# The in-place product of scattered expert weights and activations: order of the walk inside one instruction

## The reference, cut to what matters

```
s = einsum('thpc,hpnc->thpn', q, keys)           # 8 heads, 2 x 128 sub-keys
sv, si = top_k(s, 16);  cv, ci = top_k(all 16 x 16 sums, 16)
eid = e1 * 128 + e2;    g = softmax(cv)          # 16384 experts
a = einsum('td,thkd->thk', xb, u_tab[eid])
coef = g * gelu(a)
y = einsum('thk,thkd->td', coef, v_tab[eid])
```

## Time and profile before

| | us |
|---|---|
| median of the runs | 4343.08 |
| span of the profiled execution | 4344.9 |
| TensorE busy | 4117.4 (95%) |
| VectorE busy | 2832.0 (65%) |
| ScalarE busy | 1848.2 (43%) |
| GpSimd busy | 701.0 (16%) |
| L1320, 128 spreads | 167.3 |
| L474, 256 operations | 557.0 |

### The profile page before, as it was taken

The page is one execution under the profiler, slowest core; times in us unless marked ns, Lnnn a source line. Parts: engine busy times, 40 slices in busy tenths (PEclk is TensorE's granted clock), DMA queues, the critical chain, the costliest instruction groups (busy, mean ns, idle before and its releaser), DMA issues.

```text
span 4344.9 us, 90772 instructions
## 1 busy us (share of the span) xinstructions
PE 4117.4 (95%) x34860; PEld 4038.3 (93%) x34860; DVE 2832.0 (65%) x3745; ACT 1848.2 (43%) x2326; POOL 701.0 (16%) x397
## 2 busy tenths in 40 slices
PE   8999999989998899999999999999989988899998
PEld 7999999988998899999898899999989988899998
DVE  4554778789559965444545555878897489755444
ACT  4444444433443344444444444444434533344443
POOL 1211000054114510000002010000353045300000
PEclk9999999999999999999999999999999999999999
DMA  5455566644553356555554456666544533465554
GB/s 177 144 162 173 174 183 181 180 131 134 171 160 121 125 172 194 181 182 183 160 150 129 145 167 181 182 181 183 150 131 145 182 127 121 135 201 183 183 182 152
DMA packets 193647, 705.65 MB, mean 162 GB/s; under 512 B 21808, under 2 KB 22000, under 8 KB 193184
## 3 DMA queue, kind: packets, MB, share of 16 engines
q1 hardware_dynamic: 190224, 692.21, 51.8%
q0 software_dynamic: 3344, 12.32, 0.7%
HBM read 698.16 MB, written 6.29 MB: 162 GB/s over the span
## 4 chain that ended last, share of the span: by engine, by line
PE 78%; DVE 9%; POOL 5%; issue 4%; DMA 3%; ACT 1%; DVEq 0%; SPq 0%; POOLq 0%; ACTq 0%
PE ps L1424 24%; PE ps L1425 24%; PE ps L1426 24%; POOL hot L474 4%; DVE w_lo L938 4%; DMA w_raw<-in_v_tab 2%; PE ps L1777 1%; DMA w_raw<-in_dense 1%; DVE key L1334 1%; DVE hot L1338 1%; DVE big L1320 1%; DVE big L998 1%; ACT w_hi L505 1%; PE ps L1687 0%; PE ps L1686 0%
## 5 line engine op out<-in xcount | busy, mean ns | idle before, releaser
L1424 PE MATMUL ps<-act_lo_t,w_hi 128*128 128x256 f32 x10112 | 2924.6, 289 | 67.3 <-DVE act_lo_t L987 36.8
L1425 PE MATMUL ps<-act_hi_t,w_lo 128*128 128x256 f32 x10112 | 2890.4, 286 | 0.0
L1426 PE MATMUL ps<-act_hi_t,w_hi 128*128 128x256 f32 x10112 | 2888.5, 286 | 0.0
L938 DVE TENSOR_TENSOR w_lo<-w_raw,w_hi 128x1024 fp32r<-128x1024 f32 x1312 | 1834.9, 1400 | 1368.9 <-ACT w_hi L505 1358.3
L505 ACT ACTIVATE w_hi<-w_raw 128x1024 fp32r<-128x1024 f32 x1312 | 1388.4, 1059 | 1845.9 <-DMA w_raw<-in_v_tab 1004.1
L1424 PEld LDWEIGHTS ps<-act_lo_t,w_hi 128*128 128x128 f32 x10112 | 1969.7, 195 | 83.4 <-issue 50.6
L1425 PEld LDWEIGHTS ps<-act_hi_t,w_lo 128*128 128x128 f32 x10112 | 1971.5, 195 | 0.1
L1426 PEld LDWEIGHTS ps<-act_hi_t,w_hi 128*128 128x128 f32 x10112 | 1970.0, 195 | 0.0
L474 POOL TENSOR_TENSOR hot<-key,jw 128x768 bf16<-128x768 bf16 x256 | 557.0, 2181 | 1672.5 <-DVE key L1334 1672.5
L1777 PE MATMUL ps<-hot,hot 128*128 128x64 bf16 x3072 | 137.8, 196 | 115.4 <-POOL hot L474 114.9
L858 ACT ACTIVATE big<-ps 128x256 f32 (+1 forms) x256 | 98.6, 385 | 320.6 <-PE ps L1426 320.2
(11 more groups left out here) (218 smaller groups left out, 1345.6 us busy)
## 6 DMA issues: line engine op xcount, KB each, us to landing
w_raw<-in_u SPq DMA_DIRECT2D x512, 512.0 KB, 3.5
w_raw<-in_v_tab SPq DMA_DIRECT2D x512, 512.0 KB, 3.7
w_raw<-in_dense SPq DMA_DIRECT2D x288, 512.0 KB, 3.6
x_spill<-big POOLq DMA_DIRECT2D x16, 256.0 KB, 4.8
big<-x_spill POOLq DMA_DIRECT2D x16, 256.0 KB, 4.4
big<-in_xT SPq DMA_DIRECT2D x4, 512.0 KB, 5.3
big<-in_keys POOLq DMA_DIRECT2D x2, 1024.0 KB, 10.4
out<-big SPq DMA_DIRECT2D x4, 512.0 KB, 2.7
```

Of the source, the lines that this page charges most:

```text
L938: dve.tensor_tensor(w_lo[:, slot, :], w_raw[:, slot, :], w_hi[:, slot, :].bitcast(F32), ALU.subtract).then_inc(s_lo, 1)
L1424: pe.matmul(out, wh, xl, start=start, stop=False, **kw)
L1425: pe.matmul(out, wl, xh, start=False, stop=False, **kw)
L1426: return pe.matmul(out, wh, xh, start=False, stop=stop, **kw)
```

## The change

One instruction gets other access patterns. `spread` multiplies the same 512 elements by the same 512 weights in the same place, and stands in the same place of the queue. Before, it walks over 8 tokens outside and 64 blocks inside: the inner step in the grid is 256 floats, and PSUM is read from front to back. After, it walks over 64 blocks outside and 8 tokens inside: the grid is read and written in runs of 8 neighbouring floats, and the inner step in PSUM is 64 floats (256 bytes). No other instruction, wait or buffer is touched, and the order of instructions is the same on every engine.

```diff
                 def spread(part, i, k):

                     dve.wait_ge(s_hot_free, i * 8 + (sc_turns(layer, part) * 8 + 2 * (k + 1) + 2))
-                    grid = at(HALF * T * part, HALF * T).rearrange("p (e t) -> p t e", t=T)
+                    grid = at(HALF * T * part, HALF * T).rearrange("p (e t) -> p e t", t=T)
                     t0 = i * SC_TOKENS + 8 * k
-                    dst = grid[:, t0:t0 + 8, :] if isinstance(i, int) else grid[:, bass.ds(t0, 8), :]
-                    dve.tensor_tensor(dst, dst, bank(4 + k, 512, 8), ALU.mult).then_inc(s_g, 1)
+                    dst = grid[:, :, t0:t0 + 8] if isinstance(i, int) else grid[:, :, bass.ds(t0, 8)]
+                    dve.tensor_tensor(dst, dst, bank(4 + k).rearrange("p (t e) -> p e t", t=8),
+                                      ALU.mult).then_inc(s_g, 1)
```

## The result

The changed kernel takes 4268.68 us (median of four runs, 4266.19 to 4271.9) against 4338.91 us in the same comparison: a ratio of 0.9838, 95% interval [0.9823, 0.9853]. That is 1.6% faster, about 70 us. The spans of the two profiled executions differ by 80.4 us (4344.9 and 4264.5); the profiled execution of the kernel before is one of its longer ones, and so this difference is larger than that of the medians. The forecast had been 29 us, and 4268.68 us is the very edge of its range (4268 to 4376).

A forecast was written before the change was run, and what follows sets the result against it. VectorE was taken to set the pace between TensorE's stalls in the four scatter stages. 48 x 0.61 = 29 us off 4344.9 us gave 4316 us, or 4314 us for the median; range 4268 to 4376 us.

The forecast's parts named there:

- Price of one spread: VectorE's spread in the four scatter stages: 0.70 us instead of 1308 ns, 0.61 us less each.
- The rival with the dearer PSUM step: PSUM read inside the spread: the wide step costs more than SBUF's, spread 1.74 us, +35 us, 4378 us; chance 0.20.
- the one of the same price: Spread: PSUM's step costs what SBUF's does, spread 1.2 to 1.3 us, 0 to 5 us less, 4340 us; chance 0.28.
- Cheap and refusals about as now: Scatter stages: spread shorter, GpSimd operations late behind VectorE (36 counted) stay; 29 us less, 4314 us; chance 0.35.
- 48 of 128 spreads on the path: Scatter stages: only 48 shortened spreads reach the end, 48 x 0.61 = 29 us; TensorE's backlog covers the other 80.
- Refusals vanish: Rival in the scatter stages: no late GpSimd operations, every pair at VectorE's pace, 57 us less, 4286 us; chance 0.10.
- VectorE's busy time down by 78 us: Sign on VectorE: its busy time falls by 78 us, the span by less than half of that.
- The 204 us that can be had: Four scatter stages: TensorE's 136 us idle plus 68 us of lowered clock, the most that can be gained there.

The follow-up runs named there:

- the run with PSUM in its own order: The changed kernel with the weights read from PSUM front to back, so each element gets another element's weight; span 4267.7 us against 4264.5 us.
- the padded run: The changed kernel with an unused sum over one PSUM bank ahead of each spread, about the old spread's length together; span 4343.6 us.
- the sum behind the wide spread: The kernel before with an unused sum over a PSUM bank between each wide spread and the key row; span 4382.2 us.
- The spread behind the hot row: Spread moved from ahead of the key row to behind the hot row (L1338): 4192.08 us in the changed kernel, 4196.01 us in the kernel before.
- the wide read alone: The kernel before, spread cut to 4 tokens, reading the grid with the wide step and writing whole runs to another buffer; span 4270.9 us.

## Why the prediction was right or wrong

*Price of one spread: right.* I took 0.70 us with 0.68 us as the lower end, and 674 ns were measured; the run with PSUM in its own order shows that the step there is free. The rival with the dearer PSUM step, and the one of the same price, are excluded. The Trainium skill's PSUM rule (Advanced Engine Details and Errata, section "Memory Cachelines") is written for matmuls and does not carry over to VectorE's read: 674 ns with the step, 675 ns without. Its SBUF rule would have each access that changes the line pay, and that agrees: 596 to 728 ns for 256 elements against 416 ns.

*"Cheap and refusals about as now": wrong, and with it the forecast.* This step held the late operations fixed, and I gave the case in which they vanish only 0.10, on the ground that the spread stays in place. It was not the place: a spread without a wide step brings none, whether short (the change) or padded to the old length (the padded run), and a wide walk brings them at half its length too (17 and 16 in two runs). What I had read as a race of small shifts was bound to the pattern that the change takes away. The two single runs point to the wide read as the part that does it.

*"48 of 128 spreads on the path": wrong for a kernel without late operations, which the change makes.* I priced the spreads that release GpSimd, and those in short cycles, at nothing, because TensorE has a backlog there. With the late operations still there (41), the sum behind the wide spread brings 37 to 48 of its 77 us to the end: half or more, where my count has 38%. That is one run, and it lengthens instead of shortening. Without late operations all of it arrives: from the changed kernel to the padded one the spans grow by 79.1 us for 128 x 0.60 = 77 us. The change takes the late operations away, so the second case holds. What remains is what the late operations themselves had cost, and by the padded run (4343.6 against 4345.5 us, one run of each) that was nothing in the sum. So the whole shortening counts: 128 x (1308 - 674) ns = 81 us, against 80.4 us between the two spans and 70 us between the medians. That the spans agree to 1 us is in part luck: from first to last key row of the four stages 69 us were saved, where 120 spreads make 76; the other 11 us lie outside, where the 8 spreads at the stages' ends make 5 and nothing in the runs explains the rest.

*"Refusals vanish", 57 us: the mechanism right, the size short, by 23 us in the spans and 13 us in the medians.* Its pair times were measured nearly as stated (7.35 for 7.38, 8.01 for 8.03 us). The term that failed is the count: I set 32 full pairs (235 and 256 us) against stretches that hold, from first key row to last, half a pair less (230.5 and 253.6 us), 13 us in all, and left out the 11 us outside.

*VectorE's busy time down by 78 us: wrong.* It rose by 10 us. The spreads take 81 us less, as priced. But the late operations had spared VectorE standing still in L938, and that came back, 109 us of it. The key rows take 14 us less (122.4 and 108.0 us), since some of them had stood still behind the operation that follows a late one.

*The 204 us that can be had: consistent.* (The third term, 68 us for the clock, comes to 70 us from the earlier trace rows.) The spread behind the hot row reaches 4196 us with the old walk, 150 us under the kernel before, with nothing touched but the place of one instruction in four stages.

What stays open: why, after a wide read, VectorE's subtraction can go ahead of a GpSimd operation that was issued before it. The runs give a condition and not the mechanism: a wide read ahead of key row, hot row and subtraction, with or without a sum behind it, but not where the spread stands behind the hot row. Even then only some are late (37 of 120 in the kernel before). And half the length brought half as many, nearly all in part 1, which no run here explains.

## What to carry to other kernels

Where a VectorE instruction reads PSUM, put the wide step there (shown for a read with a step of 256 bytes) and keep runs of neighbouring elements on its SBUF side; then look at what stands around it, because an instruction with a PSUM operand can be free altogether in the time in which GpSimd locks the others out. When two engines both look like the limit in turns, measure a stall by taking it away at equal length before pricing it: here 37 late operations cost nothing, and in single runs such operations were a small loss beside a shorter instruction and a gain beside a longer one. And a disturbance that always follows one instruction should be tied to that instruction's form in the forecast, not only to its place.

## What the runs showed of the hardware that I had not expected

- VectorE read PSUM with an inner step of 256 bytes at full rate: 674 ns for 512 elements, 675 ns from front to back.
- In SBUF an inner step of 1024 bytes cost 180 ns for 256 elements when only read, 186 ns when only written, 312 ns when both.
- A wide read ahead of instructions with two SBUF operands let them keep GpSimd out, in spite of its earlier start, mostly until the next spread, which has a PSUM operand: 5.59 us for an operation of 1.70 us. In three of the 37 cases of the kernel before it came in sooner, while VectorE waited for another engine (3.8 us), and once, with the wide read alone, ahead of a key row (3.17 us). With a wide write or no wide step this was seen in none of 256 operations per run. The Trainium skill (SBUF — State Buffer, section "SBUF: two separate sides") has the lock go to whichever starts first; the runs without a wide read agree with it, the others do not.
- An instruction with one operand in PSUM and in-place data in SBUF ran beside a GpSimd operation at its own speed: 0.68 us with runs of 8, 1.36 us with the wide step.
